# P V in two halves over two attention steps, forget gates in column groups, and a reordered first unit in a two-layer hybrid trunk

## Chip, cores and metric

One core of one Trainium2 chip. The metric is the device time of one launch in microseconds (us), the median of several runs. Engines: PE is TensorE, ACT is ScalarE, DVE is VectorE, POOL is GpSimd, SP issues most DMAs.

## What is computed

`x` is 512 tokens by 1024 features, float32. Layer 0: a half-step SwiGLU (width 2816), then a mixer, then a second half-step SwiGLU. Layer 1 has a short gated convolution in the mixer's place. Every block starts with an RMS norm over the features. The mixer of layer 0 reads one projection for two branches:

```python
u, g, q, k, v, f_logit = split(h @ w_in)          # 512, 512, 512, 512, 512, 8 columns
a = silu(rmsnorm(conv31(u * sigmoid(g)) + b))     # depthwise, 31 taps
log_f = log_sigmoid(f_logit + b_f); cum = cumsum(log_f)          # 8 heads
logits = q k^T / 8 + cum[query] - cum[key], causal
o = softmax(logits) @ v                           # 8 heads of 64
x = x + concat(a, o) @ w_out
```

## The kernel before, in words

**Layout.** `x` lies in SBUF with features on the partitions: 8 row tiles of 128 by 512 tokens (`KD` = 8). A projection unit is a 128-column weight tile, split into a high and a low part, times the split activations: 8 row tiles by 3 matmuls of 128x512 (`product`, L1322 to L1326; `projection`, L1339). A weight tile is loaded by SP into one of four `raw` slots, ACT copies its rounded high part (`w_hi`, L645), DVE subtracts for the low part (`w_lo`, L964). `w_hi` and `w_lo` have two slots, so a split of unit i waits until unit i-2 is multiplied. Each engine's instructions run strictly in the order in which the code issues them; semaphores are the only link between engines.

**Start.** PE turns the 8 tiles of `x` (`turn_x`, L1401) into five PSUM banks; ACT writes `xg_hi` from the bank (`first_high`), DVE writes `xg_lo` (`first_low`) and copies the bank to `x` (`first_copy`, L1244); ACT squares `x` (`first_square`, L670) into two buffers, POOL adds the squares one after the other (`add_squares`, L492). A square waits for the add of two squares before. Before the change the squares are interleaved with the `xg_hi` of the first unit. After unit 1 PE sums the squares over partitions (L1389), which starts the chain that gives `rstd`: DVE mean, ACT Ln and Exp, DVE refinement, then the gate of pair 0 (L1042).

**Gate and up projections of the convolution (`A_GATE`).** Eight units in two groups of four. Between unit 6 and unit 7 PE computes the forget gates: the 8 columns of weights, repeated at four partition offsets (`wf_hi`, `wf_lo`), as 24 matmuls of 128x512 into bank 5. ACT's order in the second group is: split of unit u+2, then the sigmoid of a pair, then some taps of the depthwise convolution (`conv_taps`, L804). For u = 3 the split is that of the second q/k unit, which waits for the end of unit 7. POOL adds the tap products (L513) and is busy with them until the attention begins; half of the taps are DVE's (L1000).

**q/k and v units.** Head norms are fanned out to 128 rows by small matmuls (`fan`, L1585, 4 rows deep, at row offset 32 times n) and DVE scales q and k (`qk_scale`, L1129). Of the fans of the second half, one stands after each of four steps of the v units (`V_FANS`). The scores of the first pair follow in v unit 2 and wait for all eight scalings.

**Attention.** 16 steps, each with one query block of 128 of a pair of heads, in the order of blocks 3, 2, 1, 0, then tail steps up to t = 20. Within step t each engine issues:

- PE: `scores(t)`; P V of a chunk at t = 5, 7, 9, ... (`weigh`, L1546; a chunk is two query blocks of a pair of heads); transposes of the probabilities of step t-2 (`turn`, L1530).
- ACT: at t = 8, 12, 16, 20 the copy of a finished output (`cat_hi`, L837), which waits for the chunk of the second half of that pair of heads; then the copy of transposed probabilities of step t-3 out of PSUM (`pt`, L847); then the exponentials of step t (L857). In four steps a weight split comes first (`NEXT_SPLIT`).
- DVE: reciprocal and scaling of the even tile of step t-1, then the maxima of step t (L1180), then the low part of an output.
- POOL: scaling of the odd tile of step t-1 (L607).

The transposes of step t-2 on PE wait for the `pt` copies of step t-3, because they share banks 4 and 5. In the last four steps PE also has parts of the output projection (`merge_part`).

Of the kernel before, what the change touches and what calls it, by code (L numbers as in the profile page):

```python
# [28 lines left out]
P = 128  # L29
# [37 lines left out]
def trunk(nc, t_in, out):  # L67
# [109 lines left out]
    TURN_BANKS = (1, 2, 3, 4, 5)  # L177
    first_rows = at("first_rows", [FIRST, P], f32, H + TB * D * 4)
# [7 lines left out]
    wf_hi, wf_lo = at("wf_hi", [P, KD, P], f32r, VAT), at("wf_lo", [P, KD, P], f32r, VAT + KD * P * 4)  # L186
# [54 lines left out]
    TAPS_V, TAPS_T = [2, 2, 2, 2, 2, 3, 4], 0  # L241
# [15 lines left out]
    QK_FANS, V_SUMS, V_FANS = {6: 0, 7: 2}, (0, 0), [(1, 2), (1, 3), (2, 0), (2, 1)]  # L257
# [42 lines left out]
    with ExitStack() as ctx:  # L300
        bank = [ctx.enter_context(nc.psum_tensor(f"bank{i}", [P, S], f32)) for i in range(BANKS)]

        def sem(name):
# [23 lines left out]
        wf_cleared, wfhi_ready, wflo_ready, f_done = (  # L327
            sem("wf_cleared"), sem("wfhi_ready"), sem("wflo_ready"), sem("f_done"))
# [28 lines left out]

        def gate_cols(tensor):

            return tensor[:, :, :].rearrange("p k (r c) -> p k r c", r=4)[:, :, :, 0:HEADS]  # L360
# [96 lines left out]
        def _(pool):  # L457
# [101 lines left out]
            for ph in phases:  # L559
# [62 lines left out]
        def _(act):  # L622
# [42 lines left out]
            def first_square(j):  # L665

                act.wait_ge(x_new, j + 1)
                if j >= 2:
                    act.wait_ge(sq_added, j - 1)
                act.activation(sq[:, j % 2, :], x[:, j, :], ACT.Square).then_inc(sq_ready, 1)  # L670
# [22 lines left out]
            def pair(ph):  # L693
                def group(g):
                    first = isinstance(g, int) and g == 0
                    for u in range(4):
# [5 lines left out]
                        if ph is A_GATE and first and u == 3:  # L702

                            act.wait_ge(wf_arrived, 16 * 5)
                            act.wait_ge(wf_cleared, 2)
                            act.activation(gate_cols(wf_hi), wf_raw[:, :, :].unsqueeze(2).broadcast_to([P, KD, 4, HEADS]),
                                           ACT.Copy).then_inc(wfhi_ready, 1)
# [229 lines left out]
        def _(dve):  # L937
# [72 lines left out]
            def pair(ph):  # L1010
                def group(g):
                    first = isinstance(g, int) and g == 0
                    for u in range(4):
                        f, half = g * 2 + u // 2, u // 2
                        if ph is A_GATE and not first and u == 0:

                            dve.wait_ge(wfhi_ready, 1)
                            dve.tensor_tensor(gate_cols(wf_lo),
                                              wf_raw[:, :, :].unsqueeze(2).broadcast_to([P, KD, 4, HEADS]),
                                              raws(gate_cols(wf_hi)), ALU.subtract).then_inc(wflo_ready, 1)  # L1020
# [162 lines left out]
            def attention(ph):  # L1183
# [6 lines left out]
                qk_scale(4)  # L1190
                conv_taps(TAPS_V[2])
                qk_scale(5)
                conv_taps(TAPS_V[3])
                split_lo(ph, 0, 3)
                qk_scale(6)
                conv_taps(TAPS_V[4])
                qk_scale(7)
                conv_taps(TAPS_V[5])

                for t in range(STEPS):  # L1200
# [23 lines left out]
                    if t >= 2:  # L1224
                        conv_taps(TAPS_T, late=t >= LAST_IN_BANK)
# [16 lines left out]
            def first_copy(j):  # L1242

                dve.tensor_copy(x[:, j, :], bank[TURN_BANKS[j % len(TURN_BANKS)]][:, :]).then_inc(x_new, 1)  # L1244

# [3 lines left out]
            for j in (0, 1):  # L1249
                first_low(j)  # L1250
# [433 lines left out]
```

## Time and profile before

| | us |
|---|---|
| median of 3 runs | 1849.33 (1849.28 to 1849.39) |
| the profiled execution | 1849.31 |
| its span | 1847.5 |
| PE busy | 1835.4 |
| DVE busy | 824.3 |
| ACT busy | 633.2 |
| POOL busy | 356.7 |

The span runs from the first to the last instruction; 1.8 us of the time lie around it. A PE record ends later than the next one starts, since matmuls are pipelined: what a matmul costs is the distance from start to start, not its duration. In the timeline a row with xN merges N records.

### The profile page before, as it was taken

How to read it: one execution, taken by the hardware profiler on the slowest of the kernel's cores; microseconds unless marked ns; L12 is line 12 of the kernel's file. 1: busy time of each engine (PE TensorE's matmuls, PEld its weight loads, DVE VectorE, ACT ScalarE, POOL GpSimd, SP SyncE). 2: the span in 40 equal slices, each digit the busy share in tenths (PEclk: the TensorE clock that was granted, in tenths of full speed). 3: DMA queues.
4: the chain of work that ended last, by engine and by line, in shares of the span. 5: the costliest groups of instructions: out<-in, count | busy, mean ns of one | idle time of the engine just before them, and what ended most of it. 6: DMA issues, size and time to landing. Idle time of an engine off the chain costs nothing.

```text
span 1847.5 us, 22267 instructions
## 1 busy us (share of the span) xinstructions
PE 1835.4 (99%) x8269; PEld 1504.5 (81%) x8269; DVE 824.3 (45%) x934; ACT 633.2 (34%) x833; POOL 356.7 (19%) x295
## 2 busy tenths in 40 slices
PE   8999999999999999999999999999999999999999
PEld 7888888888668888888888888888888888888887
DVE  6343433368856443443344343333455544343321
ACT  5333322247765333332233333222212333333221
POOL 5111111129853111111111111011213221111000
PEclk9999999999999999999999999999999999999999
DMA  5333343233104333333323333432333333333331
GB/s 162 103 91 102 91 125 94 77 80 92 35 24 126 101 93 98 95 114 105 88 79 95 99 93 100 121 94 81 92 91 103 91 102 92 102 91 110 108 111 35
DMA packets 341403, 174.85 MB, mean 95 GB/s; under 512 B 6304, under 2 KB 340332, under 8 KB 341356
## 3 DMA queue, kind: packets, MB, share of 16 engines
q1 hardware_dynamic: 337100, 172.12, 32.2%
q10 hardware_dynamic: 4256, 2.11, 0.4%
q8 instruction: 29, 0.48, 0.1%
q14 instruction: 18, 0.15, 0.0%
HBM read 172.10 MB, written 2.10 MB: 94 GB/s over the span
## 4 chain that ended last, share of the span: by engine, by line
PE 93%; DVE 4%; ACT 2%; issue 1%; POOL 0%; ACTq 0%; DVEq 0%; POOLq 0%
PE bank L1324 30%; PE bank L1326 30%; PE bank L1325 30%; DVE w_lo L964 1%; DVE conv L1000 1%; ACT w_hi L645 1%; ACT tap_prod L804 0%; PE bank L1530 0%; DVE neg_max L1180 0%; PE bank L1546 0%; ACT probs_a L857 0%; PE bank L1465 0%; DVE k_n L1129 0%; PE bank L1515 0%; DVE q_n L1129 0%
## 5 line engine op out<-in xcount | busy, mean ns | idle before, releaser
L964 DVE TENSOR_TENSOR w_lo<-raw,w_hi 128x1024 fp32r<-128x1024 f32 (+2 forms) x308 | 408.5, 1327 | 697.0 <-ACT w_hi L645 696.5
L1324 PE MATMUL bank<-xg_hi,w_hi 128*128 128x512 f32 x1728 | 673.8, 390 | 2.7 <-DVE w_lo L964 2.6
L1326 PE MATMUL bank<-xg_hi,w_lo 128*128 128x512 f32 x1728 | 672.3, 389 | 0.0
L1325 PE MATMUL bank<-xg_lo,w_hi 128*128 128x512 f32 x1728 | 672.3, 389 | 0.0
L645 ACT ACTIVATE w_hi<-raw 128x1024 fp32r<-128x1024 f32 (+2 forms) x308 | 339.9, 1104 | 775.6 <-PE bank L1326 775.5
L1324 PEld LDWEIGHTS bank<-xg_hi,w_hi 128*128 128x128 f32 x1728 | 324.3, 188 | 72.7 <-DVE w_lo L964 3.1
L1326 PEld LDWEIGHTS bank<-xg_hi,w_lo 128*128 128x128 f32 x1728 | 324.3, 188 | 67.6
L1325 PEld LDWEIGHTS bank<-xg_lo,w_hi 128*128 128x128 f32 x1728 | 324.4, 188 | 66.9 <-issue 0.2
L545 POOL TENSOR_TENSOR scaled<-acted,rstd 128x512 f32<-128x512 f32 x92 | 118.8, 1291 | 835.9 <-ACT acted L722 787.9
L1324 PE MATMUL bank<-h_hi,w_hi 128*128 128x512 f32 x704 | 274.5, 390 | 0.0
L1326 PE MATMUL bank<-h_hi,w_lo 128*128 128x512 f32 x704 | 274.0, 389 | 0.0
L1325 PE MATMUL bank<-h_lo,w_hi 128*128 128x512 f32 x704 | 273.9, 389 | 0.0
L492 POOL TENSOR_TENSOR sq_sum<-sq_sum,sq 128x512 f32<-128x512 f32 x48 | 77.0, 1605 | 426.0 <-ACT sq L657 416.5
L1326 PEld LDWEIGHTS bank<-h_hi,w_lo 128*128 128x128 f32 x704 | 132.1, 188 | 27.7
L1325 PEld LDWEIGHTS bank<-h_lo,w_hi 128*128 128x128 f32 x704 | 132.2, 188 | 27.4
L1324 PEld LDWEIGHTS bank<-h_hi,w_hi 128*128 128x128 f32 x704 | 132.1, 188 | 27.0
L722 ACT ACTIVATE acted<-gate 128x512 f32<-128x512 f32 x92 | 58.1, 632 | 187.5 <-DVE gate L1042 187.5
L727 ACT ACTIVATE h_hi<-hid 128x512 f32 (+1 forms) x88 | 55.7, 632 | 178.6 <-DVE hid L1049 178.6
L1052 DVE TENSOR_TENSOR h_lo<-hid,h_hi 128x512 f32 (+1 forms) x88 | 60.9, 692 | 78.0 <-ACT h_hi L727 78.0
L513 POOL TENSOR_TENSOR conv<-conv,tap_prod 128x511 f32<-128x511 f32 (+29 forms) x60 | 81.6, 1360 | 8.4 <-POOL conv L513 0.4
L1094 DVE SCALAR_TENSOR_TENSOR x<-bank,x 128x512 f32<-128x512 f32 (+1 forms) x32 | 22.1, 692 | 127.3 <-PE bank L1326 127.3
L1042 DVE TENSOR_TENSOR gate<-bank,rstd 128x512 f32<-128x512 f32 x100 | 68.3, 683 | 0.2
(193 smaller groups left out, 991.9 us busy)
## 6 DMA issues: line engine op xcount, KB each, us to landing
raw<-in_ffn_w_gate SPq DMA_DIRECT2D x88, 512.0 KB, 3.8
raw<-in_ffn_w_up SPq DMA_DIRECT2D x88, 512.0 KB, 3.8
raw<-in_ffn_w_down SPq DMA_DIRECT2D x64, 704.0 KB, 4.5
raw<-in_od_w_in SPq DMA_DIRECT2D x24, 512.0 KB, 3.7
raw<-in_ev_w_in SPq DMA_DIRECT2D x20, 512.0 KB, 3.8
raw<-in_ev_w_out SPq DMA_DIRECT2D x16, 256.0 KB, 2.8
raw<-in_od_w_out SPq DMA_DIRECT2D x8, 512.0 KB, 3.9
x_rows<-in_x SPq DMA_DIRECT2D x4, 512.0 KB, 6.7
```

The source lines that it names most:

```text
L492: pool.tensor_tensor(sq_sum[:, :], sq_sum[:, :], sq[:, half, :], ALU.add)\
L513: pool.tensor_tensor(conv[:, b, shift:S], conv[:, b, shift:S], tap_prod[PROD_HOME[p]][:, 0:S - shift], ALU.add).then_inc(tap_added, 1)
L545: pool.tensor_tensor(scaled[:, :], src[:, par, :], rstd[:, :], ALU.mult).then_inc(gate_ready, 1)
L645: act.activation(w_hi[:, u % 2, c0:c0 + n], raw[:, u % 4, 0:n], ACT.Copy).then_inc(whi_ready, 1)
L722: act.activation(acted[:, par, :], gate[:, par, :], func).then_inc(gate_acted, 1)
L727: act.activation(h_hi[:, bass.ds(f, 1), :], hid[:, :], ACT.Copy).then_inc(hhi_ready, 1)
L964: dve.tensor_tensor(w_lo[:, u % 2, c0:c0 + n], raw[:, u % 4, 0:n], raws(w_hi[:, u % 2, c0:c0 + n]), ALU.subtract).then_inc(wlo_ready, 1)
L1042: dve.tensor_tensor(gate[:, half, :], bank[u][:, :], rstd[:, :], ALU.mult)\
L1052: dve.tensor_tensor(h_lo[:, one, :], hid[:, :].unsqueeze(1), raws(h_hi[:, one, :]), ALU.subtract).then_inc(hlo_ready, 1)
L1324: pe.matmul(dst, a[0], b[0], start=start, stop=False)
L1325: pe.matmul(dst, a[0], b[1], start=False, stop=False)
L1326: return pe.matmul(dst, a[1], b[0], start=False, stop=stop)
```

## The change

P V of a chunk is cut into two halves by key blocks. The first is issued at step 5 + 2 chunk, the second one step later, before the transposes. The forget gates are computed by 8 float32 matmuls with 32 weight columns each, which go to four column groups of bank 5 (two row tiles per group), from the unsplit `x` and the weights times the norm's gains (`wf_gain`, made by POOL). ACT copies the four partial sums to SBUF, and after unit 7 one matmul with a 128x128 matrix of ones at equal row modulo 32 (`same_head`, made by POOL) adds them. The four single fans of the v units become two pairs. Four DVE taps move from before the attention into steps 3 to 6. In the first unit the weight split comes before the copies of `x`, most squares come after the split of unit 1, and the sum of squares moves from after unit 1 into the middle of unit 2.

```diff
+    COPIES = [0, 1, 2, 5, 6, 7, 3, 4]
-    TAPS_V, TAPS_T = [2, 2, 2, 2, 2, 3, 4], 0
+    TAPS_V, TAPS_T = [2, 2, 3, 3, 3], 1
-    ... V_FANS = [(1, 2), (1, 3), (2, 0), (2, 1)]
+    ... V_FANS = {(1, 2): AB, (2, 0): AB + 2}
 # POOL, before A_GATE
-                    pool.memset(raws(wf_hi[:, :, :]), 0.0).then_inc(wf_cleared, 1)
-                    pool.memset(raws(wf_lo[:, :, :]), 0.0).then_inc(wf_cleared, 1)
+                    pool.memset(wf_gain[:, :, :], 0.0).then_inc(wf_ready, 1)
+                    pool.memset(same_head[:, :], 0.0).then_inc(same_ready, 1)
...
+                    pool.tensor_tensor(wf_gain[:, :, 0:HEADS], wf_raw[:, :, :],
+                                       gains.unsqueeze(2).broadcast_to([P, KD, HEADS]), ALU.mult).then_inc(wf_ready, 1)
+                    for n in range(7):
+                        pool.wait_ge(same_ready, n + 1)
+                        pool.affine_select(out=same_head[:, :], ...).then_inc(same_ready, 1)
 # ACT, pair(), after split_hi(ph, g, u + 2)
-                        if ph is A_GATE and first and u == 3:
-                            act.activation(gate_cols(wf_hi), wf_raw ..., ACT.Copy).then_inc(wfhi_ready, 1)
+                        if ph is A_GATE and not first and u == 3:
+                            act.wait_ge(f_parts, 1)
+                            act.activation(lf[3][:, :], bank[5][:, :], ACT.Copy).then_inc(f_copied, 1)
 # ACT, start
             for j in (0, 1):
                 first_high(j)
+            split_hi(phases[0], 0, 0)
             first_square(0)
-            split_hi(phases[0], 0, 0)
             for j in (2, 3):
                 first_high(j)
+            first_square(1)
             for j in range(4, KD):
-                first_square(j - 3)
                 first_high(j)
             split_hi(phases[0], 0, 1)
-            for j in (KD - 3, KD - 2, KD - 1):
+            for j in range(2, KD):
                 first_square(j)
 # DVE: the subtraction for wf_lo goes; V phase and start
                 conv_taps(TAPS_V[1])
                 qk_scale(4)
+                qk_scale(5)
                 conv_taps(TAPS_V[2])
-                qk_scale(5)
-                conv_taps(TAPS_V[3])
                 split_lo(ph, 0, 3)
                 qk_scale(6)
-                conv_taps(TAPS_V[4])
                 qk_scale(7)
-                conv_taps(TAPS_V[5])
+                conv_taps(TAPS_V[3])
...
-                        conv_taps(TAPS_V[6])
+                        conv_taps(TAPS_V[4])
+                        value(3)
                         maxima(1)
-                        value(3)
...
-                    if t >= 2:
+                    if t >= 3:
                         conv_taps(TAPS_T, late=t >= LAST_IN_BANK)
...
             for j in (0, 1):
                 first_low(j)
+            split_lo(phases[0], 0, 0)
+            for j in (0, 1):
                 first_copy(j)
-            split_lo(phases[0], 0, 0)
-            for j in range(2, KD):
+            for j in (2, 3):
                 first_low(j)
-                if 3 <= j < KD - 1:
-                    first_copy(j - 1)
+            first_copy(2)
+            for j in range(4, KD):
+                first_low(j)
+            first_copy(3)
             split_lo(phases[0], 0, 1)
-            for j in (KD - 2, KD - 1):
-                first_copy(j)
+            for n in range(4, KD):
+                first_copy(n)
 # PE
+                        if first and ph is phases[0] and u:
+                            pe.wait_ge(x_new, u + 3)
...
+                            hook = late_squares if u else turn_in
                         projection(ph, g, u, wait_x=first and u == 0, before=hook)
                         if ph is A_GATE and not first and u == 2:
-                            pe.wait_ge(wflo_ready, 1)
+                            pe.wait_ge(wf_ready, 2)
                             for k in range(KD):
-                                last = product(bank[5][:, :], (wf_hi[:, k, :], wf_lo[:, k, :]),
-                                               (xg_hi[:, k, :], xg_lo[:, k, :]), k == 0, k == KD - 1)
-                            last.then_inc(f_done, 1)
+                                rows = slice(k % 4 * F_COLS, (k % 4 + 1) * F_COLS)
+                                last = pe.matmul(bank[5][rows, :], wf_gain[:, k, :], x[:, k, :], start=k < 4, stop=k >= 4)
+                            last.then_inc(f_parts, 1)
+                        if ph is A_GATE and not first and u == 3:
+                            pe.wait_ge(same_ready, 8)
+                            pe.wait_ge(f_copied, 1)
+                            pe.matmul(bank[5][:, :], same_head[:, :], lf[3][:, :], start=True, stop=True).then_inc(f_done, 1)
                         if first and u == 1 and ph is phases[0]:
-                            sum_squares(ph)
...
+            def late_squares(k):
+                if k == KD // 2:
+                    sum_squares(phases[0])
...
-                def weigh(chunk):
+                def weigh(chunk, part):
...
+                    half = HALF_ROWS[c] // 2
+                    if part == 0:
+                        pe.wait_ge(pt_ready, 4 * chunk + 4)
+                        if c == 0 and j >= 2:
+                            pe.wait_ge(olo_ready, j - 1)
+                    for kb in range(part * half, (part + 1) * half):
...
-                    last.then_inc(pv_done, 1)
+                    if part == 1:
+                        last.then_inc(pv_done, 1)
...
-                    chunk = every(t, PV_AT, 2, CHUNKS)
-                    if chunk is not None:
-                        weigh(chunk)
+                    for part in (1, 0):
+                        chunk = every(t, PV_AT + part, 2, CHUNKS)
+                        if chunk is not None:
+                            weigh(chunk, part)
```

## Rows read from the trace of the kernel before

**Rows 1.** The page: busy time of each engine and its share of the span.

```profile
PE 1835.4 (99%) x8269; PEld 1504.5 (81%) x8269; DVE 824.3 (45%) x934; ACT 633.2 (34%) x833; POOL 356.7 (19%) x295
```

**Rows 2.** Timeline of the start: start us, duration us, engine, line, operation [idle before].

```profile
6.07 1.48 ACT L662 ACTIVATE xg_hi<-bank,vec 128x512 fp32r<-128x512 f32 x2 [3.22 <-PE bank L1412]
...
9.87 1.46 DVE L964 TENSOR_TENSOR w_lo<-raw,w_hi 128x1024 fp32r<-128x1024 f32 x1 [0.39 <-ACT w_hi L645]
...
19.83 0.50 PE L1324 MATMUL bank<-xg_hi,w_hi 128*128 128x512 f32 x1 [0.64 <-DVE w_lo L964]
...
21.39 1.30 POOL L492 TENSOR_TENSOR sq_sum<-sq_sum,sq 128x512 f32<-128x512 f32 x1 [0.47 <-ACT sq L670]
...
22.85 2.15 POOL L492 TENSOR_TENSOR sq_sum<-sq_sum,sq 128x512 f32<-128x512 f32 x1 [0.16 <-POOL sq_sum L492]
```

**Rows 3.** Timeline of the end of unit 1 and of the chain from the squares.

```profile
25.40 1.02 PE L1389 MATMUL bank<-sq_sum,ones 128*128 128x512 f32 x2
...
26.35 0.47 PE L1324 MATMUL bank<-xg_hi,w_hi 128*128 128x512 f32 x1
26.46 0.69 DVE L1031 TENSOR_SCALAR mean_sq<-bank 128x512 f32<-128x512 f32 x1 [2.60 <-PE bank L1389]
...
31.54 0.69 DVE L1042 TENSOR_TENSOR gate<-bank,rstd 128x512 f32<-128x512 f32 x1
...
33.88 2.18 DVE L964 TENSOR_TENSOR w_lo<-raw,w_hi 128x1024 fp32r<-128x1024 f32 x1 [1.65 <-ACT w_hi L645]
...
40.29 1.47 DVE L964 TENSOR_TENSOR w_lo<-raw,w_hi 128x1024 fp32r<-128x1024 f32 x1 [1.65 <-ACT w_hi L645]
```

**Rows 4.** Timeline of the forget gates, unit 7 and the first q/k unit.

```profile
414.13 0.39 PE L1324 MATMUL bank<-xg_hi,wf_hi 128*128 128x512 f32 x1
...
419.57 0.39 PE L1324 MATMUL bank<-xg_hi,w_hi 128*128 128x512 f32 x1
...
420.41 2.52 ACT L804 ACTIVATE tap_prod<-a_in,conv_w 128x505 f32<-128x505 f32 x4
...
425.02 0.60 PE L1624 MATMUL bank<-ident,rstd 128*128 128x128 f32 x4
425.27 1.06 ACT L645 ACTIVATE w_hi<-raw 128x1024 fp32r<-128x1024 f32 x1 [2.34 <-PE bank L1326]
```

**Rows 5.** Timeline of the v units: four head sums, and single fans.

```profile
473.14 0.60 PE L1595 MATMUL bank<-sq,head_sel 128*4 128x512 f32 x2
...
474.11 0.19 PEld L1324 LDWEIGHTS bank<-w_hi,xg_hi 128*128 128x128 f32 x1 [0.86 <-ACT qk_raw L907]
...
482.50 0.50 PE L1585 MATMUL bank<-head_rows,fan_rows 4*128 4x512 f32 x1
482.93 0.50 PE L1324 MATMUL bank<-w_hi,xg_hi 128*128 128x512 f32 x1
```

**Rows 6.** Timeline of the entry into the attention.

```profile
492.85 0.50 PE L1508 MATMUL bank<-cum_r,row_sel 64*128 64x512 f32 x2 [0.88 <-DVE k_n L1129]
...
503.09 0.39 PE L1508 MATMUL bank<-cum_r,row_sel 64*128 64x256 f32 x2 [0.51 <-DVE v L1172]
```

**Rows 7.** Timeline of attention steps 8 to 11: ACT's output copy, PE's blocks.

```profile
516.61 0.60 ACT L837 ACTIVATE cat_hi<-bank 128x512 fp32r<-128x512 f32 x1
517.09 0.88 ACT L847 ACTIVATE pt<-bank 128x384 f32<-128x384 f32 x2
...
519.54 0.69 ACT L857 ACTIVATE probs_a<-bank,neg_max 128x512 f32<-128x512 f32 x1 [1.57 <-DVE neg_max L1180]
...
524.28 1.06 PE L1530 MATMUL bank<-ident,probs_a 128*128 128x128 f32 x8 [0.45 <-ACT pt L847]
...
526.14 0.63 PEld L1546 LDWEIGHTS bank<-pt,v 128*64 128x64 f32 x8
...
526.95 0.64 PEld L1530 LDWEIGHTS bank<-ident,probs_a 128*128 128x128 f32 x6 [0.17 <-issue]
...
527.57 0.59 ACT L837 ACTIVATE cat_hi<-bank 128x512 fp32r<-128x512 f32 x1
```

More of the change, by code:

```diff
@@ L185, in trunk @@
     v = at("v", [P, TB, ATT], f32, VAT)
-    wf_hi, wf_lo = at("wf_hi", [P, KD, P], f32r, VAT), at("wf_lo", [P, KD, P], f32r, VAT + KD * P * 4)
+    F_COLS = P // 4
+    wf_gain, same_head = at("wf_gain", [P, KD, F_COLS], f32, VAT), at("same_head", [P, P], f32, VAT + KD * F_COLS * 4)
     CAT = VAT + 2 * TB * ATT * 4
@@ L584, in _ @@
                     pool.wait_ge(unit_done, ph.unit0)
[L585 to L586 removed]
+                    pool.memset(wf_gain[:, :, :], 0.0).then_inc(wf_ready, 1)
+                    pool.memset(same_head[:, :], 0.0).then_inc(same_ready, 1)
+                    pool.wait_ge(wf_arrived, 16 * 5)
+                    pool.wait_ge(vec_ready, 2)
+                    pool.wait_ge(wf_ready, 1)
+                    gains = vec[:, GAIN_COL[ph.norm]:GAIN_COL[ph.norm] + KD]
+                    pool.tensor_tensor(wf_gain[:, :, 0:HEADS], wf_raw[:, :, :],
+                                       gains.unsqueeze(2).broadcast_to([P, KD, HEADS]), ALU.mult).then_inc(wf_ready, 1)
+                    for n in range(7):
+                        pool.wait_ge(same_ready, n + 1)
+                        pool.affine_select(out=same_head[:, :], in_=same_head[:, :], compare_op=ALU.not_equal, fill=1.0,
+                                           base=(n - 3) * F_COLS, pattern=[[-1, P]], channel_multiplier=1)\
+                            .then_inc(same_ready, 1)
                 if ph.kind == "pair":
@@ L663, in first_high, with first_square @@
                                scale=vec[:, j + GAIN_COL[0]:j + GAIN_COL[0] + 1]).then_inc(xhi_ready, 1)
[L665 to L670, printed above, removed]
+            def first_square(n):
+                act.wait_ge(x_new, n + 1)
+                if n >= 2:
+                    act.wait_ge(sq_added, n - 1)
+                act.activation(sq[:, n % 2, :], x[:, COPIES[n], :], ACT.Square).then_inc(sq_ready, 1)
             logs = [0]
@@ L1014, in group @@
                         f, half = g * 2 + u // 2, u // 2
[L1015 to L1020, printed above, removed]
                         if not (first and u in (1, 2)):
@@ L1532, in turn @@
                         last.then_inc(probs_turned, 1)
-                def weigh(chunk):
+                def weigh(chunk, part):
                     j, c = chunk // 2, chunk % 2
-                    pe.wait_ge(pt_ready, 4 * chunk + 4)
-                    if c == 0 and j >= 2:
-                        pe.wait_ge(olo_ready, j - 1)
-                    for kb in range(HALF_ROWS[c]):
+                    half = HALF_ROWS[c] // 2
[4 more added lines that the diff above has]
+                    for kb in range(part * half, (part + 1) * half):
                         last_row = kb == HALF_ROWS[c] - 1
@@ L1657, in _ @@
                             elif (u, tb) in V_FANS:
-                                fan(AB + V_FANS.index((u, tb)))
+                                fan(V_FANS[u, tb])
+                                fan(V_FANS[u, tb] + 1)
                             if (u, tb) in V_SCORES:
```

18 lines of the change are left out of this document (6 added, 12 removed).

## The prediction, made before the changed kernel was run

> **What bounds the kernel.** I read the page first: PE is busy for 1835 of 1847.5 us and nothing else is over half busy [rows 1]. So the kernel is PE's order of work plus the few places where PE waits. Next I read PE's waits and then the timeline around the four places that the change touches: the first two units, the forget gates, the fans with the entry into the attention, and the attention steps. In each the reader is to look for two things: how far apart PE's starts lie, and what each engine that PE will wait for is doing when PE arrives. The sum is made against the profiled execution, 1849.3 (span 1847.5 plus 1.8 around it), which is the median to within 0.02.
>
> The change is good for PE's own work nearly everywhere. What decides is that it moves three steps of ScalarE (ACT) behind something late in its in-order queue, and PE waits for each.
>
> **Part 1, the start.** Before, the split of unit 0 waits for a square, DVE subtracts from 9.87 to 11.33, and PE multiplies. After, the split may start at 7.55, when the second `xg_hi` ends [rows 2]; 1.06 for it (the split at 425.27 [rows 4]) and about 1.25 for the subtraction (it ran 1.46 beside an add of POOL) give a first product at 9.9, 1.5 earlier. Unit 1 waits for its own split, which now comes right behind the last `xg_hi`: I follow the order and get 18.45 against 19.83 [rows 2], a gain of 1.4. Its end is then 24.0, and with the two small transposes PE could start unit 2 at 24.45.
>
> But unit 2's split stands in ACT behind all squares. Only two squares come before the split of unit 1, where six did. Squares 2 and 3 end at 17.3 and 17.85; from there POOL has adds 2 to 5 to do before square 7 may start. An add is 1.30 alone and 0.16 to the next, and 2.0 to 2.15 beside a weight subtraction [rows 2]. One long and three short ones: 17.35 + 2.1 + 3 x 1.46 = 23.8. Square 0.6, split 1.05, subtraction 1.4: unit 2 starts at 26.9 against 26.35 [rows 3], although PE was free 1.9 earlier. The sum of squares (0.86 before: 25.40 to the next instruction at 26.26) now lies in unit 2, so unit 3 starts 0.55 + 0.95 = 1.5 later than before.
>
> The chain behind the sum starts later too: its matmul goes from 25.40 to about 29.7, mean to gate takes 5.1 before [rows 3], less 0.9 since a table load is no longer in its way, so the gate of pair 0 moves from 31.54 to 35.0. Behind it on ACT is the split of unit 4, whose subtraction ended at 36.06; now, with less overlap with POOL, at 39.1, for a unit due at 38.85. From there it is 5.7 to the next such subtraction (36.06 to 41.76 [rows 3]) against 5.45 for a unit, which costs another 0.2. **Term: +1.8.** Bounds: -1.4 if the squares are never late; +3.5 if the four adds all take 2.
>
> **Part 2, forget gates.** Removed: 24 matmuls, 414.13 to 419.57, 5.44 [rows 4]. Added: 8 float32 matmuls in four column groups. Four head sums of the same kind, also at offsets 0, 32, 64 and 96, take 0.97 together including the change of shape [rows 5], while one float32 128x512 matmul takes 0.86 [rows 3]; so four groups overlap. Two rounds of 0.86 and 0.3 for the change of shape: 2.05. Unit 7 then ends at 414.13 + 2.05 + 5.45 = 421.6. PE now waits for ACT's copy. That stands behind the split of the second q/k unit, and that one waits for unit 7's end and for four taps that ran until 422.93 [rows 4], since the gate before them was DVE's to give and DVE was behind PE. The removed `wf_lo` subtraction brings these forward by 0.34: split 422.6 to 423.65, copy to 424.2, the `same_head` matmul (0.86) to 425.1. Before, PE was at that point at 425.02. **Term: +0.1**; PE waits for 2.6 where it had saved 2.5. Bounds: -2.6 if the copy is not waited for, +0.8. POOL's new work (two memsets, a small product, seven selects) lies in its idle time before the gates; under it about 9 us are free. The q/k phase starts with ACT and DVE some 2 us ahead, which hides nothing that PE waits for.
>
> **Part 3, fans and entry.** A single fan costs 0.43 to the next product [rows 5] and about 0.2 more at its ends; a pair of them runs in one slot, 0.6. Two slots less: -1.26. PE then waited 0.88 for the last scaling at 492.85 [rows 6]; the scalings now come without taps between them and end near 490.6, so the scores start about 2 earlier. Most of that is lost again: the first transposes need POOL's scaling of an odd tile, and POOL adds taps without a gap until 500.04 whatever PE does. They end near 501.8, where scores(2) started at 503.09 after a wait of 0.51 for a `v` copy [rows 6]. **Term: -1.0**, bounds -2.2 (POOL's taps get shorter) and -0.3. The four DVE taps in steps 3 to 6, 0.74 each, fit in the 0.8 that DVE idles per step; at step 6 one delays a reciprocal by 0.6, ahead of a step in which ACT has room.
>
> **Part 4, P V.** The work is the same; a block of 8 records takes 0.81 from its first start to the transposes behind it, of which 0.64 is work and 0.17 the turn [rows 7]. Eight more blocks: 6 x 0.17 in the loop and two between products of the output projection at about 0.45: +1.9. Gained: the steps without P V had PE wait for the `pt` copies, 0.45 at 524.28 [rows 7], four such waits (0.28 to 0.46) of which three now have a half block in front: -1.3.
>
> The rule that speaks against cutting is about this turn. The Trainium skill, TensorEngine Tiling (Array Packing), section Tiling Modes, says that a change of tiling mode drains the engine, while different tiles of one mode overlap. By it each added block would pay at both of its ends, 16 x 0.17 = 2.7 in place of 1.9; the trace has the gap behind a block and none in front of it, so I keep 1.9.
>
> The dearest part is a dependence. At t = 8, 12 and 16 ACT first copies the output of a pair of heads, which waits for the whole chunk; then it copies the `pt` of step t-3, and PE's transposes in the same step t wait for that. The chunk used to be finished in step t-1, and ACT copied at 516.61, then `pt` at 517.09, and idled 1.57 before its exponential [rows 7]. Now the chunk's second half is issued by PE in step t itself, behind scores(t). PE finishes it and has only the transposes left, which wait for: tail and semaphore 0.15, output copy 0.48, first `pt` copy 0.5, and 0.17 for the second tile, less the turn that is paid anyway. That is 1.2 each, three times: +3.6 (at t = 20 there are no transposes, and the last output copy has a block of 9 products over it, 9 x 0.227 = 2.04 against the 1.5 that it needs). The exponential starts 1.0 later, and the next transposes of 8 (step t+2) meet their `pt` copy just in time. **Term: +4.2**, bounds +0.6 (the waits hidden) and +5.8.
>
> **Sum.** 1.8 + 0.1 - 1.0 + 4.2 = +5.1: 1849.3 becomes **1854.4**. About 0.2% (3.7 us) is what a measurement of this kernel tells from no change; so the forecast is slower, with little to spare.
>
> **Rivals.**
> *ACT's queue is never last (faster).* If PE reaches each of the three places later than ACT, only PE's own work counts: -1.4 - 2.6 - 2.2 + 0.6 = -5.6, 1843.7. It is decided where ACT's order meets PE: at `f_copied` after unit 7, it needs the split of the second q/k unit not to be in front of the copy. For it: PE is 99% busy and ACT 34% [rows 1]. Against it: before, that split starts 0.25 after PE ends unit 7 [rows 4], so it cannot be earlier than unit 7's end. Chance 0.12.
> *The output copy's wait is given back (no change).* The delayed steps are followed by steps in which PE itself had waited, and the loop of maxima and exponentials has slack; then +3.6 falls away or is halved: 1850.8 to 1852.6. For it: 1.57 idle before the exponential. Against it: PE's blocks, not that loop, fill the period, which is 10.96 at this place (516.61 to 527.57 [rows 7]) and 10.74 from transposes to transposes. Chance 0.28, at 1851.
> *The exponential loop becomes the bound.* The 1.0 by which the exponential is late is not caught up before the transposes of 8, 0.8 a period: +2.4, 1856.8. Chance 0.13.
> *The column groups don't overlap* when each has 32 columns of weights, not 4. Then the parts take 6.9, unit 7 ends at 426.5, and the copy comes after it: +4.1 more, 1858.5. Chance 0.04; the head sums speak against it [rows 5].
>
> **Chances.** Forecast 0.43, its own range 1853.1 to 1856. Slower by over 0.2%: 0.43 + 0.13 + 0.04 = 0.60. Within: 0.28. Faster: 0.12. The range leaves out the faster case and the last one, 0.16: it goes from 1848.5, a low end for no change with the start's bound in it, to 1857.3.
>
> **What would show it.** In the changed trace: the first unit at 9.9 and unit 1 at 18.4; unit 2 at about 26.9 with PE waiting 2 or so for `w_lo`; PE idle for 2.6 ahead of `same_head`, released by ACT; scores(0) about 2 and scores(2) about 1 earlier relative to the v units; at t = 8, 12 and 16 PE waiting about 1.1 for `pt`, and none at t = 6, 10, 14. The attention's period goes from 10.74 to about 12.0. No PE wait at `same_head`, or an unchanged period, would prove me wrong.

## The result, and the profile after

The changed kernel takes **1858.17 us** (five runs, 1858.12 to 1859.10) against 1849.33: a ratio of 1.0049 (95% interval 1.0038 to 1.0059), slower by 8.8. The forecast was 1854.4, with a range up to 1857.3. The side was right, the size was not: the cost is 8.8 where 5.1 was worked out.

The page's first lines, of the profiled execution (1858.17):

```profile
span 1856.4 us, 22273 instructions
PE 1837.2 (99%) x8263; PEld 1500.8 (81%) x8263; DVE 824.8 (44%) x933; ACT 634.3 (34%) x833; POOL 360.4 (19%) x303
```

Against [rows 1] PE has 1.8 more busy time, although the change takes matmuls away, and the span is 8.9 longer. So most of the loss is time in which PE waits. The view of PE's waits (who waits for whom: us in total, times, longest) says for whom:

```profile
PE bank L1327 <- DVE w_lo L971: 4.4, 5, 2.9
PE bank L1544 <- ACT pt L854: 4.0, 5, 1.2
PE bank L1413 <- POOL ident L466: 2.5, 1, 2.5
PE bank L1380 <- ACT lf L714: 2.3, 1, 2.3
PE bank L1544 <- POOL probs_a L616: 1.9, 1, 1.9
```

The third was there before. The others are the changed places, one by one.

**Start.** Timeline of PE, the first high product of each row tile in unit 2, and the sum of squares; then the windows around it (length, busy time and count of PE, PEld, DVE, ACT, POOL, then the granted clock, DMA share, GB/s):

```profile
18.35 0.47 PE L1327 MATMUL bank<-xg_hi,w_hi 128*128 128x512 f32 x1 [0.64 <-DVE w_lo L971]
...
27.08 0.55 PE L1327 MATMUL bank<-xg_hi,w_hi 128*128 128x512 f32 x1 [2.86 <-DVE w_lo L971]
...
28.28 0.63 PE L1327 MATMUL bank<-xg_hi,w_hi 128*128 128x512 f32 x1
...
29.56 0.63 PE L1327 MATMUL bank<-xg_hi,w_hi 128*128 128x512 f32 x1
...
31.49 1.02 PE L1398 MATMUL bank<-sq_sum,ones 128*128 128x512 f32 x2
```

```profile
24.00:27.00 3.00, 0.22 (x3) 0.03 (x1) 1.23 (x1) 2.88 (x4) 2.38 (x3) 1.00 0.00 1
27.00:29.00 2.00, 1.92 (x5) 1.58 (x6) 0.00 (x0) 0.93 (x1) 1.57 (x3) 0.58 0.20 54
29.00:31.00 2.00, 2.00 (x6) 1.55 (x6) 0.00 (x0) 0.00 (x0) 1.36 (x5) 0.56 0.70 208
31.00:33.00 2.00, 2.00 (x8) 1.31 (x7) 0.45 (x1) 0.00 (x0) 1.71 (x8) 1.00 0.00 0
```

Unit 1 at 18.35 (18.45 forecast) and unit 2 at 27.08 (26.9) are where they were put. What was not forecast stands in the last but two columns: behind 2.9 us of idleness the granted clock is 0.58 and 0.56, that is mostly the 1.2 GHz level, and the row tiles lie 1.2 to 1.3 apart where 0.68 is normal. The next place that both kernels share, the end of unit 6, comes 3.9 later (the gates' first matmul at 418.06 against 414.13 [rows 4]); 1.8 was forecast.

**Forget gates.** PE after unit 7, and ACT's copy that it waits for:

```profile
427.99 1.10 PE L1380 MATMUL bank<-lf,same_head 128*128 128x512 f32 x2 [2.30 <-ACT lf L714]
...
428.92 0.60 PE L1642 MATMUL bank<-ident,rstd 128*128 128x128 f32 x4
```

```profile
426.32 1.04 ACT L654 ACTIVATE w_hi<-raw 128x1024 fp32r<-128x1024 f32 x1
427.27 0.57 ACT L714 ACTIVATE lf<-bank 128x512 f32<-128x512 f32 x1
```

The transposes come 3.90 later than in [rows 4] (425.02): what the column groups save, the wait gives back, as forecast.

**Entry.** scores(0) at 494.41 and scores(2) at 506.13 are 1.56 and 3.04 later than in [rows 6]; with the 3.9 from the start taken off, 2.3 and 0.9 earlier (2 and 1 were forecast). In between PE waits 1.88 for POOL.

**Attention.** PE at step 8 and the three waits for ACT; ACT at step 8:

```profile
521.59 0.44 PE L1562 MATMUL bank<-pt,v 128*64 128x128 f32 x4
523.20 0.79 PE L1544 MATMUL bank<-ident,probs_b 128*128 128x128 f32 x4 [1.17 <-ACT pt L854]
...
535.26 0.79 PE L1544 MATMUL bank<-ident,probs_b 128*128 128x128 f32 x4 [1.17 <-ACT pt L854]
...
546.43 0.79 PE L1544 MATMUL bank<-ident,probs_b 128*128 128x128 f32 x4 [1.17 <-ACT pt L854]
...
562.42 0.50 PE L1327 MATMUL bank<-cat_hi,w_hi 128*128 128x512 f32 x1 [0.40 <-DVE w_lo L971]
```

```profile
522.08 0.60 ACT L844 ACTIVATE cat_hi<-bank 128x512 fp32r<-128x512 f32 x1 [0.68 <-PE bank L1562]
522.57 0.87 ACT L854 ACTIVATE pt<-bank 128x384 f32<-128x384 f32 x2
```

The output copy starts as soon as the chunk's second half is done, and PE's transposes wait for the copy behind it; before, the same two stood at 516.61 and 517.09 with the chunk long finished [rows 7]. From there the period is 12.06 (523.20 to 535.26), 12.0 by the forecast. The product that follows the last wait, 562.42, stood at 553.74: 8.68 later, of which 5.64 is the attention's; 4.2 was forecast. The wait of 0.40 in that row was not.

### The profile page after: what moved, and what is told of

The parts are those of the page before. It is cut to its first block, busy times and chain, and to the rows that moved or that the text cites. A ratio compares the mean times of both kernels' runs of the same rounds, so it can differ in the third digit from the quotient of the medians.

```text
span 1856.4 us, 22273 instructions
## 1 busy us (share of the span) xinstructions
PE 1837.2 (99%) x8263; PEld 1500.8 (81%) x8263; DVE 824.8 (44%) x933; ACT 634.3 (34%) x833; POOL 360.4 (19%) x303
## 4 chain that ended last, share of the span: by engine, by line
PE 92%; DVE 3%; POOL 2%; ACT 2%; issue 1%; ACTq 0%; POOLq 0%
PE bank L1327 30%; PE bank L1328 30%; PE bank L1329 30%; POOL conv L511 2%; DVE w_lo L971 1%; DVE conv L1007 1%; ACT w_hi L654 1%; PE bank L1544 1%; PE bank L1562 1%; ACT tap_prod L811 0%; POOL sq_sum L490 0%; PE bank L1529 0%; PE bank L1522 0%; PE bank L1479 0%; PE bank L1426 0%
```

## Experiments

All times are medians; the kernel before ran beside each group at 1849.22 to 1849.32.

### Each part alone, on top of the kernel before

The edits are the parts of the diff above, no others.

> The kernel before with the start's edits alone (order of the first unit, squares behind the split of unit 1, sum of squares in the middle of unit 2). Theory L (the ledger of the two traces: the start costs 3.9, of it 1.8 as predicted and 2.1 because TensorE's granted clock falls to 0.56 to 0.58 for four products after its 2.9 us of idleness before unit 2): 1853.2, gate parts' place (end of unit 6) 3.9 later than before, granted clock under 0.6 between 27 and 31 us. Rival S (the clock's fall belongs to the whole changed kernel or is chance, and the start by itself costs its predicted 1.8): 1851.1, clock 1.00 there.

> The kernel before with the forget gates' edits alone. Theory L (saved matmul time and the new wait for ScalarE's copy cancel, as both traces' marks say): 1849.3, PE idle 2.3 us ahead of the matmul with the matrix of ones. Rival S (POOL's nine new instructions push its taps back so that the attention's entry, which waits for POOL, comes later): 1849.8 or more, with the wait for POOL's scaling in the entry longer than in the kernel before.

> The kernel before with two pairs of fans in place of four single ones, and the moved DVE taps, alone. Theory L (two slots less and earlier scores, mostly lost again at the wait for POOL's first odd scaling): 1848.4, 0.9 less than before. Rival S (alone it gains more, since without the start's delay of 3.9 us, which POOL shares, the place where POOL's taps end relative to PE is another): 1847.3. If the four taps in steps 3 to 6 of the attention cost something there, 1849 or more.

> The kernel before with P V in two halves over two steps alone. Theory L (three waits of 1.2 for the copies behind the output copy, about 0 net from blocks and removed stalls in the loop, 2.0 in the tail of it 0.4 a wait for a weight subtraction): +5.7, 1855.0, PE waiting 1.1 to 1.2 for ScalarE's copy at steps 8, 12 and 16. Rival S (part of the 5.7 is from the four DVE taps moved into steps 3 to 6, or from the entry being earlier, and not from P V): +4.2, 1853.5, as the prediction's term has it.

| | median | executions |
|---|---|---|
| start | 1852.77, ratio 1.0017 (1.0007 to 1.0026) | 4 at 1851.8 to 1852.0, 6 at 1852.8 to 1853.0 |
| gates | 1849.18, 1.0005 (0.9995 to 1.0014) | 6 at 1849.1 to 1849.2, 4 at 1851.2 to 1851.5 |
| fans | 1849.66, 1.0001 (0.9991 to 1.0010) | 3 at 1848.7 to 1848.8, 7 at 1849.7 to 1849.9 |
| P V | 1855.09, 1.0031 (1.0020 to 1.0043) | 7 at 1855.1 |

Against 1849.27 this is +3.5, -0.1, +0.4 and +5.8, together 9.6 where the whole costs 8.8. With the fans' faster group in place of their median (-0.5 for +0.4) it is 8.7, so the parts add up. P V is 5.8 by itself, so it is its own and not the moved taps'. And three parts fall into two groups of executions 1 to 2 us apart, each of them a part with a PE wait of 1.9 us or more; P V, whose longest wait is 1.17, and the kernel before have one group. The profile of the fans fell into the slower group. Windows of it, and then PE at the wait:

```profile
499.00:501.00 2.00, 0.89 (x6) 0.52 (x5) 1.51 (x3) 0.26 (x1) 2.00 (x2) 1.00 0.00 0
501.00:502.00 1.00, 0.25 (x2) 0.25 (x3) 0.17 (x1) 1.00 (x5) 0.70 (x1) 1.00 0.00 0
502.00:504.00 2.00, 2.00 (x14) 1.08 (x12) 0.59 (x2) 1.04 (x2) 1.73 (x2) 0.64 0.04 8
504.00:506.00 2.00, 2.00 (x15) 1.68 (x14) 1.11 (x4) 1.02 (x4) 1.04 (x2) 0.51 0.00 0
```

```profile
501.75 0.66 PE L1528 MATMUL bank<-ident,probs_a 128*128 128x128 f32 x4 [1.86 <-POOL probs_a L607]
```

Behind the 1.86 the clock is 0.64 and 0.51. In the changed kernel's own profile the same wait (1.88) left it at 1.00. That is the two groups: behind the same wait the clock drops in some executions and not in others. The mean clocks agree: 0.999 in the seven slower executions of the fans, 1.000 in the three others. Without the drop the fans gain 0.5.

### One wait at a time, on top of the changed kernel

```diff
 # warm_fill: PE, behind the two small transposes after unit 1
+                            warm(12)        # 128x128 matmuls of constants into bank 6
 # split2_early: ACT, start
-            for j in range(2, KD):
-                first_square(j)
+            for j in range(2, 4):
+                first_square(j)
+            split_hi(phases[0], 0, 2)
+            for j in range(4, KD):
+                first_square(j)
 # ... and the later place of this split goes
 # f_copy_first: ACT, second group of A_GATE, u == 3
+                            act.wait_ge(f_parts, 1)
+                            act.activation(lf[3][:, :], bank[5][:, :], ACT.Copy).then_inc(f_copied, 1)
                             split_hi(ph, g, u + 2)
-                            act.wait_ge(f_parts, 1)
-                            act.activation(lf[3][:, :], bank[5][:, :], ACT.Copy).then_inc(f_copied, 1)
 # out_copy_later: ACT, attention step
-                    j = every(t, OUT_AT, TB, AB)
-                    ...
                     copied = 0 if t == PT_AT - 1 else t - PT_AT if t > PT_AT else None
                     ...
+                    j = every(t, OUT_AT, TB, AB)
+                    ...
```

> The changed kernel with 12 matmuls of 128x128 (of two constants, into bank 6, which nothing reads then) behind the two small transposes ahead of unit 2: PE is busy there in place of idle, unit 2 still waits for its weight subtraction until about 27.1. Theory C (the granted clock fell because PE stood idle for 2.9 us): clock 1.00 in unit 2, k steps 0.68 apart, 2.0 us less: 1856.1. Rival D (the clock falls there for another reason, such as all the gaps since the first product): clock again below 0.6 after 27, 1858.2.

> The changed kernel with ScalarE's split of unit 2 moved from behind all eight squares to behind the fourth. Theory C (the start's whole loss is that one split's place: idle time, fallen clock and the late chain of the first gate): PE starts unit 2 near 24.4 with clock 1.00, sum of squares near 27.2, and unit 4 starts near 36.3; the start then gains about 1.0 against the kernel before in place of losing 3.9: 1853.3. Rival D (POOL's adds are what is late; with the split in front of them the sum of squares has to be waited for in the middle of unit 2, and the gate of pair 0 is not earlier than it was): PE stands still for about 2 in unit 2, 1856.

> The changed kernel with ScalarE's copy of the partial forget gates ahead of the split of the second q/k unit, which waits for unit 7's end. Theory C (the wait before the matrix of ones is this queue order alone): the wait of 2.3 goes and PE is 2.3 earlier from there on: 1855.9. Rival D (the wait is replaced: DVE and ScalarE, no longer ahead of PE by 2.3, are late at the q/k units, or POOL's taps hold the entry to the attention where they did, as a gain in front of POOL's fixed work is lost there): gate part gains 2.3 and the entry gives up to 2 of it back, 1857.5 to 1858.

> The changed kernel with ScalarE's copy of a finished output behind the copies of transposed probabilities of the same step in place of ahead of them. Theory C (the three waits at steps 8, 12 and 16 come from this order alone, and there is room behind): the period falls from 12.05 to about 10.9 and the time by 3 x 1.17 = 3.5: 1854.7. Rival D (then the exponentials are late behind the output copy, and the loop of maxima and exponentials takes the wait's place): half of it or less, 1856.5 to 1858.

**warm_fill, 1857.99** (four runs, 1856.89 to 1858.78). The clock holds at 1.00 in unit 2, so it was the idleness. But the sum is hardly better, for two reasons. Of what the clock gave, some went into a new wait of 0.34 at unit 4 (39.28, for its weight subtraction); the gates came 1.42 earlier. And in this profile the clock fell in the entry instead, windows 504 to 508:

```profile
504.00:505.00 1.00, 0.90 (x6) 0.57 (x6) 0.59 (x2) 0.83 (x4) 0.43 (x2) 0.72 0.00 0
505.00:507.00 2.00, 2.00 (x12) 1.15 (x14) 0.22 (x1) 0.58 (x1) 2.00 (x2) 0.50 0.00 0
507.00:508.00 1.00, 1.00 (x10) 0.79 (x11) 0.54 (x2) 0.76 (x3) 0.26 (x1) 0.57 0.00 0
```

**split2_early, 1859.57**: slower than the changed kernel by 1.4, both theories missed. Unit 2 starts in time and the sum of squares waits 0.72, as the rival had it. Then POOL is late: the first gate is ready for it at 34.5, and it is still at the constants for the head norms, which it starts after the last square.

```profile
36.96 0.34 POOL L577 TENSOR_SCALAR_AFFINE_SELECT row_add<-row_add 128x128 fp32r<-128x128 f32 x1
37.27 1.28 POOL L543 TENSOR_TENSOR scaled<-acted,rstd 128x512 f32<-128x512 f32 x1
```

Unit 5 waits 1.90 for its weight subtraction (at 44.49), and the clock is 0.54 and 0.50 from there to 48; in this execution it fell in the entry too (0.50 from 506 to 508). A wait had been moved, not removed.

**f_copy_first, 1857.87** (1856.74 to 1859.05). The wait before the matrix of ones is 1.35 in place of 2.30: the copy now stands behind four taps that ACT makes until 426.2. And at 469.08 PE waits 0.82 for a weight subtraction where it had not waited; scores(0) is 0.15 earlier, all that is left. Most of the time gained is given back between these two places; what paces the queues of the head norms there was not taken apart further.

**out_copy_later, 1854.19** (1852.94 to 1856.56): of PE's waits for `pt` in the attention, one of 0.23 is left (517.39). The three of 1.17 were the order of ACT's two copies. The spread is the clock again (this profile has it fallen both in the start and in the entry), so the size is read better from the next group.

### The clock held, and P V taken apart

> The changed kernel with matmuls of two constants (128x128, into bank 6) in all three places where PE stands idle for 1.9 to 2.9 us: 12 ahead of unit 2, 10 ahead of the matrix of ones, 8 ahead of the transposes that wait for POOL. Seen so far: with the first place filled the clock stayed at 1.00 there but fell to 0.50 for 3 us in the entry, and single executions of one kernel lie 0.9, 1.0 or 2.0 us apart. Theory C (each idle stretch of 1.9 us or more can make the clock fall in an execution, and costs 1 to 2 us where it does): clock 1.00 everywhere, all executions within 0.3 us, 1856.8, which is the lowest single time with only the first place filled. Rival D (the falls are of the chip and not of the idle places): again executions 1 to 2 us apart, median 1857.9.

> The kernel before with P V in two halves only for the first six chunks; the last two, between the products of the output projection, stay whole. Theory L (of the 5.8 of P V in halves, 3.8 is the loop, by the three waits of 1.2, and 2.0 the tail: four blocks for two between products, the last output copy later, and the wait of 0.40 for a weight subtraction behind it): 1853.1, no wait at the first full unit of the output projection. Rival S (the tail's part is only the loop's delay seen late: whatever ends the loop later, the weight subtraction is late too): 1854.5 or more.

> The kernel before with P V in two halves and ScalarE's output copy behind the copies of the probabilities. Nothing of the start is in it, so the clock should hold. Theory L (waits at steps 8, 12 and 16 are the order's, 3 x 1.17, and 0.4 more from the exponentials that come earlier): 3.9 less than with the halves alone, 1851.2; what is left, 1.9, is the cost of more blocks. Rival S (what the last run with this edit gained, 3.1 by its trace, was all that there is): 1852.0. If the halves are of use at all once the wait is gone, it is under 1849.3.

```diff
 # gaps_filled: the changed kernel with warm(12) as above, and
+                            warm(10)        # ahead of the wait for f_copied
+                            warm(8)         # ahead of the transposes that wait for the first odd scaling
 # pv_loop_only: the kernel before with the split P V, and
-                        if chunk is not None:
+                        if chunk is not None and chunk < 6:
                             weigh(chunk, part)
+                        elif chunk is not None and part == 0:
+                            weigh(chunk, 0)
+                            weigh(chunk, 1)
```

**gaps_filled, 1856.88**, five runs within 0.23 (1856.82 to 1857.05), against 1856.8 forecast. Windows:

```profile
24.00:27.00 3.00, 2.90 (x27) 2.71 (x25) 1.23 (x1) 2.88 (x4) 2.38 (x3) 1.00 0.00 1
27.00:29.00 2.00, 1.92 (x9) 1.63 (x10) 0.00 (x0) 0.93 (x1) 1.58 (x3) 1.00 0.25 62
...
505.00:507.00 2.00, 2.00 (x23) 1.44 (x24) 0.88 (x3) 1.10 (x4) 2.00 (x2) 1.00 0.00 0
```

Matmuls that compute nothing make the changed kernel 1.3 faster and steady. That is what the fallen clock costs it; the other 7.6 are waits and blocks.

**pv_out_later** (the kernel before with the split P V and the edit of out_copy_later), **1851.28** (1.0011, 1.0001 to 1.0020): 3.8 less than the halves alone. ACT at step 8, the copies to `pt` done before, the output copy waiting with only the exponentials behind it:

```profile
519.10 0.60 ACT L849 ACTIVATE cat_hi<-bank 128x512 fp32r<-128x512 f32 x1 [1.56 <-PE bank L1548]
519.60 0.68 ACT L857 ACTIVATE probs_a<-bank,neg_max 128x512 f32<-128x512 f32 x1
```

So of the 5.8, 3.8 is the order of two copies and 2.0 the halves themselves: cutting P V is of no use even then. **pv_loop_only, 1853.62** (1.0023, 1.0014 to 1.0033): between the two theories. The last two chunks' cut costs 1.5, the loop 4.3; the output projection then starts at 545.95 against 541.67 and has no wait at its first full unit.

### What the start and the other drops are

> The kernel before with the start's edits and 12 small matmuls of constants in the idle time ahead of unit 2. The start alone took 1852.77 with two groups of executions, at 1851.8 and 1852.8. Theory C (the 1 us between the groups and part of the loss are the clock; the rest is the late split of unit 2 and the late chain of the first gate): steady within 0.3 us, 1851.5, 2.2 over the kernel before, and 1.8 was predicted for it. Rival D (the clock costs as much as the matmuls of unit 2 show, 2.1, since nothing later waits): 1850.8.

> The kernel before with the forget gates' edits and 10 small matmuls of constants in the idle time ahead of the matrix of ones. The gates alone had six executions at 1849.15 and four at 1851.2 to 1851.5, and the profile was of the first kind, with the clock at 1.00. Theory C (in the others the clock fell behind the 2.3 us of idleness): all executions within 0.3 us of 1849.2. Rival D (the second group is something else): it is there again in about 4 of 10.

**start_filled, 1851.85**: eight of ten executions at 1851.6 to 1852.1, the level of the faster group of the start alone (1851.8 to 1852.0); the two others, 1852.7 and 1853.2, have spans like the rest (1850.3 and 1850.1) and are longer outside the span. The clock is 0.9 of the start's 3.5; its queue order is 2.6, where 1.8 was forecast. **gates_filled, 1849.19**: nine of ten at 1849.17 to 1849.25, and none near 1851. So the 2.0 of the four others was the clock, behind an idle stretch of 2.3. None of the four was profiled: this rests on the filling and on their mean clock, 0.999 where the six others have 1.000. The part is worth nothing either way.

### A version that beats both

best1 is the kernel before with the first unit and the fans of the changed one, P V whole, the gates as before, and these orders:

```diff
 # ACT, start: a square between the high parts; two behind the split of unit 1, then the split of unit 2
+            for j in (4, 5):
+                first_high(j)
+            first_square(2)
+            for j in (6, 7):
+                first_high(j)
             split_hi(phases[0], 0, 1)
+            for j in (3, 4):
+                first_square(j)
+            split_hi(phases[0], 0, 2)
+            for j in range(5, KD):
+                first_square(j)
 # ACT, first pair: the split of unit 4 ahead of the gate's silu
                             norm_root(mean_ready, ...)
+                            if ph is phases[0]:
+                                split_hi(ph, g, 4)
 # POOL: its constants behind the gates of the first phase
                     add_squares(0)
+                    gates(ph)
 # PE: warm(8) ahead of the transposes that wait for the first odd scaling
```

> A combination meant to beat both kernels: the kernel before, with the changed first unit and the fans in pairs, P V whole and the forget gates as before. ScalarE's order in the start is new: third square before the last two high parts, fourth and fifth behind the split of unit 1, then the split of unit 2, then the other squares; the split of unit 4 stands ahead of the sigmoid of the first gate; POOL makes its constants for the head norms behind the gates of the first phase; 8 small matmuls of constants fill the wait for POOL in the entry. Theory C (the start's loss was the queue order, on ScalarE and then on POOL): unit 2 at 24.0, sum of squares at 26.7 without a wait, unit 4 at 35.8 in place of 37.34 before, then the fans' 0.55: 1847.2, clock 1.00. Rival D (the chain from the sum of squares, which starts 1.3 later than before, holds the first pairs whatever stands in front of it): unit 5 waits and the start gains nothing, 1848.7 to 1849.3.

> The kernel before with the first unit of the changed one and the new order of ScalarE and POOL from the combination that ran at 1847.37, nothing else. Its trace has scores(0) 3.8 and scores(2) 2.3 earlier than before, so the start there gave about 1.5. Theory C (the first unit's edit is worth 1.5 as soon as no queue is late behind it): 1847.8. Rival D (the combination's gain is mostly the fans' and the filled entry): 1848.7 or more.

> The combination that ran at 1847.37, without the eight filling matmuls in the entry, and with four in place of two of POOL's additions of convolution taps moved from before the attention into its steps 2 to 5. Theory P (in the entry PE waits for POOL's first odd scaling, which stands behind its taps; two additions fewer are 2.6 earlier): no wait at the first odd transposes, up to 1.5 less, 1845.9, clock 1.00. Rival V (the copies of v, the exponentials or the taps in the steps take POOL's place): 1847 or more.

**best1, 1847.37** (0.9990, 0.9981 to 0.9999). **start_order**, the start of it alone, **1847.80** (0.9992, 0.9982 to 1.0001; ten runs of 1847.6 to 1847.9 beside 31 of 1849.21 to 1849.34). The intervals come close to 1 or reach it; that these kernels are faster than the one before rests on their executions, all 31 of which (with best2's) are at 1847.9 or less. PE in the start of best1:

```profile
23.80 0.47 PE L1336 MATMUL bank<-xg_hi,w_hi 128*128 128x512 f32 x1
...
26.64 1.02 PE L1402 MATMUL bank<-sq_sum,ones 128*128 128x512 f32 x2
```

Unit 2 starts at 23.80 without a wait, 2.5 earlier than in [rows 3], and the sum of squares 1.2 later than there; since the split of unit 4 now stands ahead of the first gate's silu, and POOL is free when the gate comes, the first unit's gain of 1.5 reaches the end. It is the edit that costs 3.5 by itself, with the orders of ACT and POOL around it mended. **best2, 1847.35**, equal: two of POOL's additions fewer ahead of the attention take away the wait for POOL's first odd scaling (and the matmuls that filled it), and the rival's waits come in its place, for exponentials, scalings and `pt`, 0.4 to 0.8 each at 500.71, 502.47, 505.14, 511.15 and 517.23. POOL was last there, but by little.

## Why the prediction was wrong

Two terms of the sum failed. In the start, the step that lets PE go on at full clock behind its wait was wrong: +1.8 was forecast and 3.5 measured. In P V the mechanism was right, but the rest of the term, more blocks less removed waits, was put at +0.6 and measured 2.0, so that +4.2 became 5.8. Of the fans' -1.0, 0.5 came. With the fans' clock held, as the changed kernel's profile has it, 3.5 - 0.1 - 0.5 + 5.8 is 8.7 of the measured 8.8.

**Start, +1.8 forecast.** Its order was right to 0.2 at units 1 and 2, and its cause too, the split of unit 2 behind the squares. Two things were missed. First, the sum took PE to go on at full clock behind a wait of about 2.4: the text forecast the idleness and gave it no price beyond its length. The step that failed is the one that puts the sum's matmul at 29.7 and unit 3 1.5 later than before: it came at 31.49, and at 29.89 with the clock held. The runs put what is left of this at the end at 1.3 in the changed kernel and 0.9 in the start alone. Secondly, with the clock held the start still costs 2.6 (2.3 in the profiled execution of start_filled). The steps written down for it, 1.5, 0.25 and 0.2, add up to 1.95 and not to 1.8. In that profile unit 4 starts 1.9 later than before (39.26 against 37.34, behind a wait of 0.34 for its subtraction), unit 5 2.2 later (44.97 against 42.78), and the gates 2.4 (416.49 against 414.13). So the late chain costs a little more at each of the next subtractions than was allowed; the last 0.2 was not located. The Trainium skill, TensorE: Matmul & The Clock Gate, section Why this matters for your kernels, asks that there be no long idle gaps of PE between bursts of matmuls. The traces agree (0.56 behind 2.86), and show the same behind 1.86 (0.51 in the fans alone).

**Gates, +0.1.** Right: -0.1 alone. The wait of 2.6 was 2.3. What it left out is that this wait too can drop the clock: 2.0 in four executions of ten.

**Fans and entry, -1.0.** Right in sign where the clock holds: 0.9 gained by the marks in the changed kernel, but 0.5 alone, half of what was forecast. The same omission as in the start: 0.9 the other way in seven executions of ten. One execution of the changed kernel, 1859.10, lies that far above its others, with a mean clock of 0.998 where they have 0.999.

**P V, +4.2; measured 5.8.** The dependence, the dearest term, was right in place and size: three waits of 1.17, and 3.8 gained without them, against 3.6. The size that failed is the rest, +0.6 forecast and 2.0 measured. In the loop, a cut block costs more than the turn behind it. With the waits gone, a period has 0.45 of idleness less than in [rows 7] and is still 0.13 longer (scores to scores, 516.87 to 527.74 in pv_out_later, 10.87 against 10.74). That is 0.58 for two more blocks, 0.29 each and not 0.17. The gap in front of a block, which the prediction said the trace did not have, is there: from the last matmul of the scores to a block 0.22 (518.40 to 518.62 in the same run), to the transposes 0.12 in the kernel before (518.55 to 518.67). The Trainium skill, TensorEngine Tiling (Array Packing), section Tiling Modes, has a drain at each change of mode, and so at both ends of a block; weighed against the trace and set aside, it was nearer, and its 2.7 for all blocks would still have been too little. In the tail 1.5 were measured for 0.9 forecast; the wait of 0.40 for the weight subtraction is part of it. Here is the subtraction on DVE in the changed kernel, and then in pv_loop_only, where PE does not wait for it:

```profile
557.70 0.69 DVE L1221 TENSOR_TENSOR cat_lo<-bank,cat_hi 128x512 fp32r<-128x512 f32 x1 [10.47 <-ACT cat_hi L844]
...
560.74 5.02 DVE L971 TENSOR_TENSOR w_lo<-raw,w_hi 128x512 fp32r<-128x512 f32 x3 [0.29 <-ACT w_hi L654]
```

```profile
556.91 0.81 DVE L964 TENSOR_TENSOR w_lo<-raw,w_hi 128x512 fp32r<-128x512 f32 x1 [2.37 <-ACT w_hi L645]
```

The prediction held the last output copy to be covered by a block of 9 products. PE's products covered it. But DVE's norm of the convolution stands behind that output, and POOL's products with the norm's result stand behind that: they start at 560.53, 0.21 ahead of the subtraction, where in pv_loop_only they start 2.3 ahead of it (554.63). The first of the three merged subtractions then takes 1.63, not 0.81, and PE waits. DVE's queue is not what holds it: DVE is idle for 0.29 ahead of it, until ACT's split is done. P V alone and pv_out_later have the same picture (1.62 and 1.63, PE waits 0.4), and the kernel before has that of pv_loop_only (0.81, no wait). That POOL's product beside it is what makes the subtraction longer is read from these five traces and was not tested by itself.

**Rivals.** None of the four came. The rival that the output copy's wait is given back was wrong: nothing of it was. The exponentials were not the bound either; with the order mended they wait for the output copy without harm.

## What to carry to other kernels

An instruction that waits for something late belongs behind everything in its queue that others need soon; here one such order cost 3.8 us, and mending another turned the same edit from +3.5 into -1.5. Price each new wait of TensorE twice, by its length and by what the clock may do behind it, look for two groups among the executions, and where the wait can't be removed, fill it with matmuls. And follow a gain to the next place where engines meet: four times here a mended wait came back at another place.

## What the runs showed of the hardware

The granted clock fell to 0.50 to 0.64 for some 3 to 4 us behind idle stretches of PE of 1.86 us (seven executions of ten in the fans alone) and 2.9 us (six of ten in the start alone). The profiled executions show the fall, and the other ones are counted by their times and mean clocks. Behind 2.3 us (four of ten in the gates alone) only times and mean clocks show it: every profile with that stretch has the clock at 1.00 there. It did not fall behind 1.17 us in 17 executions. A drop cost 0.9 to 2.0 us. The same idle stretch of the same program dropped the clock in one execution and not in the next, so a single profile shows only one of the two.
